# Eight memory query blocks moved from the stick-breaking stage's filler to the opening stage's quarter products

## The chip, the cores and the metric

The kernel runs on one core of a Trainium2 chip. TensorE (PE) multiplies matrices, VectorE (DVE), ScalarE (ACT) and GpSimd (POOL) do the elementwise work, and SyncE (SP) issues the DMAs. Each engine works through its own list of instructions in order and waits for the others at semaphores. The metric is the time of one execution in microseconds (us), lower is better.

## What is computed

One decoder layer on 1024 tokens of width 1024, in float32. The input is normed (RMSNorm gives `u`) and multiplied by one combined matrix `w_in`; the columns of the product feed three branches:

```python
u = rms_norm(h, norm_mix_pre)
proj = u @ w_in
sb_qkv, z, xbc_raw, dt_raw, mem_q, gate_logits = jnp.split(proj, SPLIT_POINTS, axis=-1)
...  # stick-breaking attention on sb_qkv; SSD on z, xbc, dt
kv = rms_norm(mem, norm_mem) @ w_mem_kv          # cross-attention into 256 memory tokens
y_mem = softmax(mem_q @ k.T / 16) @ v
...  # three projections, merged by sigmoid gates, w_o, norm, residual, squared-ReLU MLP
# ssd_branch:
xbc = silu(causal_depthwise_conv(xbc_raw, conv_w, conv_b))      # 4 taps
y = ssd_chunked(...) * silu(z)
```

`w_in` is held as 96 blocks of 128 columns. Blocks 0 to 23 are q, k, v of the stick-breaking attention, 24 to 39 are `z`, 40 to 63 are `xbc`, 64 to 71 are `mem_q`, 72 to 95 are the gates.

## The kernel before

Every float32 product is made of three passes over rounded halves (`split3`: high times high, high times low, low times high), so that a full product of one block of `w_in` with all 1024 tokens is 8 x 3 x 2 = 48 matmuls of 128x512.

**The opening stage** (`front`). DVE norms ten tiles of 128 tokens (eight of `x`, two of the memory). For tile i these are `invert(i)` (L854 and L858: the reciprocal and the scaled tile), then PE's `turn(i)` (L553, eight transposes), `scale_turned(i)` (L870), ACT's `round_u(i)` (L716), and `rest_of_u(i)` (L876). PE multiplies blocks 0 and 1 while the tiles come (`piece`, L562, two tiles at a time) and the dt columns (`decays`, L650), then sixteen memory items (`product_of_memory`, L576, 24 matmuls each). The weight of such an item is rounded by ACT (`round_kv`, L737) and its rest made by DVE (`rest_of_kv`, L894). Beside these items stand the four sums of `u` quarters that the next part multiplies (`round_t` L758 on ACT and `rest_of_t` L901 on DVE, in items 1 to 4), and after item 15 the first weights' halves (`round_front`, `round_back` L781, `rest_of_front` L905, `rest_of_back` L913).

Then come blocks 2 to 23 in eleven pairs. A pair is a 2 x 2 grid of quarters and is multiplied by seven quarter products in place of eight (`PRODUCTS`, L583): 7 x 4 x 3 = 84 matmuls of 128x512 a pair instead of 96. POOL makes four weight sums a pair, ACT rounds, DVE makes the rests and adds up the results.

**The stick-breaking stage** has 8 pairs of heads with 16 steps each, 128 steps in all. In step i, with t = i mod 8, PE multiplies scores on (t+1) x 128 columns (L1301); ACT takes two sigmoids (L1395 and L1399), DVE scans one of them (L1509), POOL multiplies (L1451), and in step i+2 PE transposes the result in one or two units (L1260), each of which ACT rounds (L1362) and DVE subtracts (L1459, `lo`). Every fourth step the values are weighed (L1317). PE transposes unit u only when DVE has finished unit u-2 (`pe.wait_ge(lo_done, u - 1)`).

Between these PE is filled with blocks of `w_in`: 48 blocks in the pattern `kinds = "xzxzxq"`, six to a pair of heads (L1279). The number of filler matmuls in a step is read from `AT_STEP`, by t. An x block goes through the convolution on DVE (`convolve`, four taps, L1469 and three times L1473, in the first and second step after the block's end), a sigmoid on ACT three steps after, a multiplication on DVE four steps after (`silu`, L1479), and a store by SP five steps after. A z block's two halves get a sigmoid from ACT (L1380) and a multiplication from DVE (`silu_of_gate`, L1484) in the step in which they end. A q block (`mem_q`) is copied by ACT (L1378) and stored. POOL splits the weights of each block (L1429, L1437). Results go through the two slots of `out_tile`, slot m mod 2 for filler block m: before, x blocks always have slot 0 and z and q blocks slot 1. A block may write its slot only when the block two before it has been stored.

After this stage come the SSD, the merge and the MLP, which the change doesn't touch.

## Time and profile before

| | |
|---|---|
| time, median of 3 runs | 2694.46 us (2691.84 to 2698.86) |
| the profiled execution | 2688.13 us, its span 2686.4 us |
| PE / DVE / ACT / POOL busy, of the span | 97% / 69% / 44% / 49% |
| granted clock of PE, mean | 0.99 |

In the profile a line such as L1279 is a line of the kernel before; "busy" of matmuls counts each until its modelled end, so a group's mean of 0.40 us is not the distance between two matmuls in a row. The chain that ended last is given by the page as PE for most of its length.

### The profile page before, as it was taken

The numbers are of one execution on the slowest core, as the hardware profiler recorded it, in microseconds if no ns is written. First come the engines' busy times: TensorE is split into PE (matmuls) and PEld (weight loads), VectorE is DVE, ScalarE is ACT, GpSimd is POOL, SyncE is SP. The second block draws the span as 40 slices with busy tenths as digits, with TensorE's granted clock in tenths as the row PEclk, the third lists the DMA queues.
The fourth block names the chain that finished last, engine by engine and source line by source line (L and its number), as shares of the span: only waits on it lengthen the run. The fifth ranks groups of instructions, "written<-read, shape, count | busy, mean of one in ns | idle before, by whom it ended". The sixth has DMA issues, their size and how long they took to land. (4 is left out here: it accounts for less than half of the span.)

```text
span 2686.4 us, 35512 instructions
## 1 busy us (share of the span) xinstructions
PE 2597.0 (97%) x12752; PEld 2175.4 (81%) x12752; DVE 1850.0 (69%) x2063; ACT 1191.2 (44%) x2098; POOL 1313.1 (49%) x809
## 2 busy tenths in 40 slices
PE   7999999999999999799999899999998999999998
PEld 6888888888888888688888777878887788888886
DVE  5666476777677677498888656653258887768567
ACT  5533144444444444467666544443144222244443
POOL 3233255454554554288888743545600676535224
PEclk9999999999999999899999999999999999999999
DMA  4634443433324341467666653434331444376574
GB/s 160 204 151 160 153 149 105 126 102 109 112 94 134 110 119 62 137 175 210 196 207 202 226 189 133 152 134 149 126 126 55 150 160 166 129 245 211 203 253 146
DMA packets 208108, 411.53 MB, mean 153 GB/s; under 512 B 19648, under 2 KB 100160, under 8 KB 207936
## 3 DMA queue, kind: packets, MB, share of 16 engines
q1 hardware_dynamic: 207936, 409.27, 46.0%
q8 instruction: 104, 1.70, 0.3%
q14 instruction: 68, 0.56, 0.1%
HBM read 289.01 MB, written 120.19 MB: 152 GB/s over the span
## 5 line engine op out<-in xcount | busy, mean ns | idle before, releaser
L1451 POOL TENSOR_TENSOR sb_beta<-sb_beta,sb_rest 128x128 f32<-128x128 f32 (+7 forms) x128 | 164.1, 1282 | 371.4 <-DVE sb_rest L1509 371.4
L1279 PE MATMUL sb_psg<-uh,sb_wl 128*128 128x512 f32 x768 | 309.7, 403 | 0.0
L1279 PE MATMUL sb_psg<-ul,sb_wh 128*128 128x512 f32 x768 | 304.3, 396 | 0.0
L1279 PE MATMUL sb_psg<-uh,sb_wh 128*128 128x512 f32 x768 | 302.8, 394 | 0.0
L3169 PE MATMUL ff_ps<-ff_mh,ff_total 128*128 128x512 f32 x896 | 278.6, 391 | 4.6 <-DVE ff_total L3672 4.6
L1509 DVE TENSOR_TENSOR_SCAN sb_rest<-sb_rest 128x128 f32<-128x128 f32 (+7 forms) x128 | 187.3, 1463 | 115.1 <-ACT sb_rest L1395 114.8
L3169 PEld LDWEIGHTS ff_ps<-ff_mh,ff_total 128*128 128x128 f32 x896 | 169.4, 189 | 41.0 <-issue 5.7
L2314 PE MATMUL first_ps<-uh,mg_wh 128*128 128x512 f32 x480 | 193.3, 403 | 6.2 <-DVE ul L2519 4.9
L2314 PE MATMUL first_ps<-ul,mg_wh 128*128 128x512 f32 x480 | 188.5, 393 | 0.0
L2314 PE MATMUL first_ps<-uh,mg_wl 128*128 128x512 f32 x480 | 188.3, 392 | 0.0
L3169 PE MATMUL ff_ps<-ff_ml,ff_total 128*128 128x512 f32 x448 | 175.2, 391 | 0.0
L1362 ACT ACTIVATE sb_wth<-sb_pst 128x512 fp32r<-128x512 f32 (+1 forms) x192 | 87.3, 490 | 189.9 <-PE sb_pst L1260 186.6
L1279 PEld LDWEIGHTS sb_psg<-ul,sb_wh 128*128 128x128 f32 x768 | 144.4, 188 | 29.9
L1279 PEld LDWEIGHTS sb_psg<-uh,sb_wl 128*128 128x128 f32 x768 | 144.6, 188 | 25.4
L1279 PEld LDWEIGHTS sb_psg<-uh,sb_wh 128*128 128x128 f32 x768 | 144.9, 189 | 24.0
L1801 PE MATMUL first_ps<-uh,ssd_gwh 128*128 128x512 f32 x384 | 155.0, 404 | 5.9 <-ACT ssd_out L1866 5.0
L1801 PE MATMUL first_ps<-ul,ssd_gwh 128*128 128x512 f32 x384 | 151.5, 395 | 0.0
L1801 PE MATMUL first_ps<-uh,ssd_gwl 128*128 128x512 f32 x384 | 151.2, 394 | 0.0
L1459 DVE TENSOR_TENSOR sb_wtl<-sb_pst,sb_wth 128x512 fp32r<-128x512 f32 (+1 forms) x192 | 99.6, 546 | 74.3 <-ACT sb_wth L1362 74.3
L2292 POOL TENSOR_TENSOR merged<-merged,mg_gate 128x1024 f32<-128x1024 f32 x24 | 61.3, 2553 | 159.6 <-DVE mg_gate L2526 159.6
L1473 DVE SCALAR_TENSOR_TENSOR sb_out<-sb_padded,sb_cw,sb_out 128x1024 f32<-128x1024 f32 x72 | 131.7, 1829 | 1.7
L1395 ACT ACTIVATE sb_rest<-sb_psz 128x128 f32<-128x128 f32 (+7 forms) x128 | 83.6, 653 | 108.6 <-PE sb_psz L1301 107.7
(422 smaller groups left out, 7259.6 us busy)
## 6 DMA issues: line engine op xcount, KB each, us to landing
sb_w<-in_w_in SPq DMA_DIRECT2D x48, 512.0 KB, 4.4
scratch_proj<-sb_out SPq DMA_DIRECT2D x48, 512.0 KB, 2.9
ff_w<-in_w_down SPq DMA_DIRECT2D x96, 256.0 KB, 3.4
sb_k<-scratch_qk SPq DMA_DIRECT2D x64, 256.0 KB, 6.1
ssd_arow<-scratch_decay SPq DMA_DIRECT2D x32, 512.0 KB, 5.6
mg_gate<-scratch_proj SPq DMA_DIRECT2D x32, 512.0 KB, 3.6
ff_w<-in_w_up SPq DMA_DIRECT2D x32, 512.0 KB, 3.7
mg_w<-in_w_branch SPq DMA_DIRECT2D x30, 512.0 KB, 4.5
```

The costliest lines, as they stand in the source:

```text
L1279: last = nc.tensor.matmul(ps_g[:, h], l[:, s, k], r[:, k, h * HALF:(h + 1) * HALF], start=(k == 0 and j == 0), stop=(k == KB - 1 and j == 2))
L1362: nc.scalar.activation(out, src, ACT.Copy).then_inc(hi_done, 1)
L1395: nc.scalar.activation(rest[:, i % 3, 1:cols + 1], ps_z[:, 0:cols], ACT.Sigmoid, scale=-0.125).then_inc(keep_done, 1)
L1451: nc.gpsimd.tensor_tensor(beta[:, i % 3, 0:cols], beta[:, i % 3, 0:cols], rest[:, i % 3, 0:cols], ALU.mult).then_inc(weighted, 1)
L1459: nc.vector.tensor_tensor(out, src, hi, ALU.subtract).then_inc(lo_done, 1)
L1473: nc.vector.scalar_tensor_tensor(out_tile[:, 0], padded[:, tap:tap + S], cw[:, n, tap:tap + 1], out_tile[:, 0], ALU.mult, ALU.add).then_in ...
L1509: nc.vector.tensor_tensor_scan(kept, kept, kept, 1.0, ALU.mult, ALU.bypass).then_inc(scanned, 1)
L1801: last = nc.tensor.matmul(ps_g[:, h], l[:, s, k], r[:, k, h * HALF:(h + 1) * HALF], start=(k == 0 and j == 0), stop=(k == KB - 1 and j == 2))
L2292: nc.gpsimd.tensor_tensor(merged[:, n % KB], merged[:, n % KB], gate[:, n % 2], ALU.add).then_inc(summed, 1)
L2314: last = nc.tensor.matmul(ps[:, s, cols], l[:, k], r[:, k, cols], start=(k == 0 and j == 0), stop=(k == KB - 1 and j == 2))
L3169: done = nc.tensor.matmul(down_bank(p, local), l[:, columns(local)], r, start=(begins and c == 0 and j == 0), stop=(c == PAIRS - 1 and j = ...
```

## The change

Three things are changed.

1. The eight `mem_q` blocks leave the filler and become four more pairs of the opening stage, after the eleven of before. The filler has 40 blocks in the pattern `"xzxxz"`, five to a pair of heads, with 8 to 22 matmuls a step in place of 11 to 25. `padded` gets a second buffer, and x and z blocks now use both slots of `out_tile`.
2. DVE norms tiles in another order: `scale_turned(i)`, `invert(i+1)`, `rest_of_u(i)`, and the third tile's `invert` stands behind the first two `rest_of_u`.
3. Memory items: the rest of weight 2 is made before the results of blocks 0 and 1 are rounded off; the four sums of `u` are rounded in items 2, 5, 8 and 11, behind the item's weight; the first pair's front factor is rounded in item 13 in place of 15, and its S1, S2 and S3 in item 14 in place of after 15.

```diff
-    BLOCK_PAIRS = [(b, b + 1) for b in range(2, Z0, 2)]
+    BLOCK_PAIRS = [(b, b + 1) for b in (*range(2, Z0 + Z_EARLY, 2), *range(MQ0, G0, 2))]
+    T_ITEMS = (2, 5, 8, 11)
...
+        round_kv(2)
         hi_of_first(0)
-        round_kv(2)
...
-            if m == 15:
+            if m == 13:
                 round_front(0)
+            if m == 14:
+                for which in (S1, S2, S3):
+                    round_back(which, 0)
...
-    kinds = "xzxzxq"
+    kinds = "xzxxz"
-    AT_STEP = (11, 13, 15, 17, 19, 21, 23, 25)
+    AT_STEP = (8, 10, 12, 14, 16, 18, 20, 22)
...
-                if kind != "x" and m >= 2:
+                if kind == "z" and m >= 2:
                     act.wait_ge(g_stored[s], (m // 2) * 16)
...
-                    if n:
-                        dve.wait_ge(g_stored[0], n * 16)
-                    nc.vector.tensor_scalar(out_tile[:, 0], padded[:, 0:S], cw[:, n, 0:1], cb[:, n:n + 1],
+                    if m >= 2:
+                        dve.wait_ge(g_stored[s], (m // 2) * 16)
+                    nc.vector.tensor_scalar(out_tile[:, s], padded[:, n % 2, 0:S], cw[:, n, 0:1], cb[:, n:n + 1],
```

(`Z_EARLY` is 0.) How this stands in the engines' lists is shown at three places.

DVE, steps 14, 15 and 16 of the second pair of heads (L1509 in before and L1522 after are the scans, of 896, 1024, 128 and then 256 columns; L1459 and L1472 are `lo`; L1469, L1473 and L1482, L1486 the taps). Before:

```order
L1509 SCALAR_TENSOR_TENSOR sb_rest<-sb_rest 128x896 [waits sb_keep]
L1459 TENSOR_TENSOR sb_wtl<-sb_pst,sb_wth 128x4x128 [waits sb_hi]
L1459 TENSOR_TENSOR sb_wtl<-sb_pst,sb_wth 128x128 [waits sb_hi]
L1469 TENSOR_SCALAR sb_out<-sb_padded,sb_cw,sb_cb 128x1024 [waits sb_gstored0,sb_drained1,sb_drained0]
L1473 SCALAR_TENSOR_TENSOR sb_out<-sb_padded,sb_cw,sb_out 128x1024 [waits sb_convstep]
L1493 TENSOR_TENSOR sb_y<-sb_psy,sb_y 64x512 [waits sb_yupper,sb_ydone]
L1509 SCALAR_TENSOR_TENSOR sb_rest<-sb_rest 128x1024 [waits sb_keep]
...
L1473 SCALAR_TENSOR_TENSOR sb_out<-sb_padded,sb_cw,sb_out 128x1024 [waits sb_convstep] x2
L1509 SCALAR_TENSOR_TENSOR sb_rest<-sb_rest 128x128 [waits sb_keep]
L1459 TENSOR_TENSOR sb_wtl<-sb_pst,sb_wth 128x4x128 [waits sb_hi]
```

After:

```order
L1522 SCALAR_TENSOR_TENSOR sb_rest<-sb_rest 128x896 [waits sb_keep]
...
L1492 TENSOR_TENSOR sb_out<-sb_out,sb_sigm 128x1024 [waits sb_sigm]
L1482 TENSOR_SCALAR sb_out<-sb_padded,sb_cw,sb_cb 128x1024 [waits sb_gstored0,sb_drained1,sb_drained0]
L1486 SCALAR_TENSOR_TENSOR sb_out<-sb_padded,sb_cw,sb_out 128x1024 [waits sb_convstep]
L1497 TENSOR_TENSOR sb_out<-sb_psg,sb_out 128x512 [waits sb_zsigm0]
L1506 TENSOR_TENSOR sb_y<-sb_psy,sb_y 64x512 [waits sb_yupper,sb_ydone]
L1522 SCALAR_TENSOR_TENSOR sb_rest<-sb_rest 128x1024 [waits sb_keep]
...
L1486 SCALAR_TENSOR_TENSOR sb_out<-sb_padded,sb_cw,sb_out 128x1024 [waits sb_convstep] x2
L1497 TENSOR_TENSOR sb_out<-sb_psg,sb_out 128x512 [waits sb_zsigm1]
L1522 SCALAR_TENSOR_TENSOR sb_rest<-sb_rest 128x128 [waits sb_keep]
L1472 TENSOR_TENSOR sb_wtl<-sb_pst,sb_wth 128x4x128 [waits sb_hi]
```

A silu (L1492) and the two gate multiplications of a z block (L1497) now stand in these steps; before they held the same four taps, but neither of those.

ACT, steps 14 and 15 of the second pair of heads. L1395, L1399 and L1408, L1412 are the two sigmoids, L1362 and L1376 the rounding of the transposed units. Before:

```order
L1395 ACTIVATE sb_rest<-sb_psz 128x896 [waits sb_weighted,sb_scores]
L1399 ACTIVATE sb_beta<-sb_psz 128x896 [waits sb_turned]
L1362 ACTIVATE sb_wth<-sb_pst 128x4x128 [waits sb_ydone,sb_turned]
L1362 ACTIVATE sb_wth<-sb_pst 128x128 [waits sb_turned]
L1417 ACTIVATE sb_y<-sb_psy 64x512 [waits sb_ydone]
L1395 ACTIVATE sb_rest<-sb_psz 128x1024 [waits sb_weighted,sb_scores]
```

After:

```order
L1408 ACTIVATE sb_rest<-sb_psz 128x896 [waits sb_weighted,sb_scores]
L1412 ACTIVATE sb_beta<-sb_psz 128x896 [waits sb_turned]
L1376 ACTIVATE sb_wth<-sb_pst 128x4x128 [waits sb_ydone,sb_turned]
L1376 ACTIVATE sb_wth<-sb_pst 128x128 [waits sb_turned]
L1392 ACTIVATE sb_out<-sb_psg 128x512 [waits sb_gstored1,sb_halfdone]
L1430 ACTIVATE sb_y<-sb_psy 64x512 [waits sb_ydone]
L1408 ACTIVATE sb_rest<-sb_psz 128x1024 [waits sb_weighted,sb_scores]
```

The sigmoid of the z block's first half (L1392) now stands in step 14 and waits for the store (`gstored1`) of the x block whose silu DVE does in the same step 14.

DVE, the norm of the third and fourth tile. Before:

```order
L876 TENSOR_TENSOR ul<-fr_f_hi,uh 128x8x128 [waits fr_uhi] x2
L854 RECIPROCAL fr_stats<-fr_stats 128x1 [waits fr_rooted]
L858 TENSOR_SCALAR fr_f_sums<-fr_f_back,fr_stats 128x1024 [waits fr_turned,fr_inverted]
L870 TENSOR_TENSOR fr_f_hi<-fr_ps,fr_gains 128x1024 [waits fr_uhi,fr_rawkept,fr_usplit,fr_turned]
L876 TENSOR_TENSOR ul<-fr_f_hi,uh 128x8x128 [waits fr_uhi]
```

After:

```order
L881 TENSOR_TENSOR ul<-fr_f_hi,uh 128x8x128 [waits fr_uhi]
L859 RECIPROCAL fr_stats<-fr_stats 128x1 [waits fr_rooted]
L863 TENSOR_SCALAR fr_f_sums<-fr_f_back,fr_stats 128x1024 [waits fr_turned,fr_inverted]
L875 TENSOR_TENSOR fr_f_hi<-fr_ps,fr_gains 128x1024 [waits fr_uhi,fr_rawkept,fr_usplit,fr_turned]
L859 RECIPROCAL fr_stats<-fr_stats 128x1 [waits fr_rooted]
L863 TENSOR_SCALAR fr_f_sums<-fr_f_back,fr_stats 128x1024 [waits fr_turned,fr_inverted]
L881 TENSOR_TENSOR ul<-fr_f_hi,uh 128x8x128 [waits fr_uhi]
```

The next tile's reciprocal and scaling now stand between a tile's `scale_turned` (L875) and its `rest_of_u` (L881).

## Rows read from the trace of the kernel before

**Rows 1.** Windows: stretch, length, busy (count) of PE, PEld, DVE, ACT, POOL; clock, DMA:
```profile
126.24:336.50 210.26, 209.89 (x924) 173.47 (x925) 128.35 (x156) 63.70 (x91) 62.80 (x42) 1.00 0.43 153
338.99:1097.14 758.15, 752.81 (x3830) 633.31 (x3828) 541.82 (x519) 341.17 (x616) 377.87 (x222) 1.00 0.35 108
```

**Rows 2.** Waits of PE in the opening stage: sum of us, times, longest:
```profile
PE fr_ps L562 <- DVE ul L876: 6.8, 3, 4.4
PE fr_ps L583 <- DVE fr_fl L905: 2.8, 1, 2.8
PE fr_ps L576 <- DVE fr_fl L894: 2.6, 2, 2.4
...
PE fr_ps L583 <- DVE fr_back L913: 0.4, 1, 0.4
```

**Rows 3.** Waits of PE from 345 to 1088 us, all there are:
```profile
PE sb_psy L1317 <- DVE sb_wtl L1459: 0.4, 1, 0.4
```

**Rows 4.** The chain that ended last, a stretch of 128x512 matmuls only:
```profile
2366.69 259.09 PE ff_ps L3169 x1143
```

**Rows 5.** Timeline of PE in the opening stage: start, duration, instruction, idle before it:
```profile
46.59 0.48 PE L562 MATMUL fr_ps<-uh,fr_fh 128*128 128x256 f32 x1 [1.90 <-DVE ul L876]
...
51.07 1.03 PE L553 MATMUL fr_ps<-ident,fr_f_sums 128*128 128x128 f32 x8
51.86 0.36 PE L562 MATMUL fr_ps<-uh,fr_fh 128*128 128x256 f32 x1
...
54.82 1.04 PE L553 MATMUL fr_ps<-ident,fr_f_sums 128*128 128x128 f32 x8
```

**Rows 6.** Timeline of DVE in the opening stage:
```profile
24.83 1.23 DVE L876 TENSOR_TENSOR ul<-fr_f_hi,uh 128x1024 fp32r<-128x1024 f32 x1 [1.12 <-ACT uh L716]
...
64.84 1.22 DVE L894 TENSOR_TENSOR fr_back<-fr_w,fr_back 128x1024 fp32r<-128x1024 f32 x1
...
72.69 4.48 DVE L894 TENSOR_TENSOR fr_fl<-fr_w,fr_fh 128x1024 fp32r<-128x1024 f32 x1
```

**Rows 7.** Timeline of DVE, steps 14 to 16 of the second pair of heads:
```profile
512.94 0.89 DVE L1459 TENSOR_TENSOR sb_wtl<-sb_pst,sb_wth 128x512 fp32r<-128x512 f32 x2 [1.91 <-ACT sb_wth L1362]
513.75 2.39 DVE L1469 TENSOR_SCALAR sb_out<-sb_padded,sb_cw,sb_cb 128x1024 f32<-128x1024 f32 x1
516.17 1.28 DVE L1473 SCALAR_TENSOR_TENSOR sb_out<-sb_padded,sb_cw,sb_out 128x1024 f32<-128x1024 f32 x1
...
521.33 3.65 DVE L1473 SCALAR_TENSOR_TENSOR sb_out<-sb_padded,sb_cw,sb_out 128x1024 f32<-128x1024 f32 x2
...
525.23 1.13 DVE L1459 TENSOR_TENSOR sb_wtl<-sb_pst,sb_wth 128x512 fp32r<-128x512 f32 x2
```

**Rows 8.** Timeline of PE: the score of step 14, the transposes in step 17:
```profile
506.93 0.39 PE L1301 MATMUL sb_psz<-sb_k,sb_q 128*128 128x512 f32 x1
...
527.77 1.04 PE L1260 MATMUL sb_pst<-ident,sb_beta 128*128 128x128 f32 x8
```

**Rows 9.** DVE lines from 350 to 1088 us: duration ns min/median/max:
```profile
L1479 DVE TENSOR_TENSOR sb_out<-sb_out,sb_sigm x23: 1298/2183/2729, 380.2 to 1060.6; 128x1024 f32<-128x1024 f32 x23
```
```profile
L1484 DVE TENSOR_TENSOR sb_out<-sb_psg,sb_out x32: 676/680/685, 362.2 to 1062.0; 128x512 f32<-128x512 f32 x32
```

**Rows 10.** Timeline of DVE: a silu, and a tap that waits for its store:
```profile
380.17 2.33 DVE L1479 TENSOR_TENSOR sb_out<-sb_out,sb_sigm 128x1024 f32<-128x1024 f32 x1
...
385.61 0.81 DVE L1469 TENSOR_SCALAR sb_out<-sb_padded,sb_cw,sb_cb 128x1024 f32<-128x1024 f32 x1 [0.36 <-DMA scratch_proj<-sb_out]
```

**Rows 11.** Groups from 350 to 1088 us: ACT's sigmoid of half a z block:
```profile
L1380 ACT ACTIVATE sb_out<-sb_psg 128x512 f32<-128x512 f32 x32 | 19.1, 598 | 30.0 <-PE sb_psg L1279 30.0
```

**Rows 12.** Timeline of POOL in steps 14 and 15 of the second pair of heads:
```profile
513.19 2.39 POOL L1437 TENSOR_TENSOR sb_wl<-sb_w,sb_wh 128x1024 fp32r<-128x1024 f32 x1
```

**Rows 13.** Timeline of PE: after idling, at the first quarter product:
```profile
126.24 0.47 PE L583 MATMUL fr_ps<-uh,fr_fh 128*128 128x512 f32 x1 [2.77 <-DVE fr_fl L905]
126.54 0.40 PE L583 MATMUL fr_ps<-ul,fr_fh 128*128 128x512 f32 x1
```

99 lines of the change are left out of this document (53 added, 46 removed).

## Prediction, made before the changed kernel ran

> **What bounds the kernel now.** I read first the windows of the two stages that the change touches. In the quarter products PE is busy for 209.89 of 210.26 us, and in the stick-breaking stage for 752.81 of 758.15 us [rows 1]. Then the waits of PE: within the 128 steps, from 345 to 1088 us, it waited once, for 0.4 us [rows 3]. So PE sets the length of both stages, and a matmul taken out is worth its distance to the next one. That distance is best read from a long stretch without a wait: 1143 matmuls in 259.09 us [rows 4], 0.2267 us each. In the opening stage PE does wait: 6.8 us for the rests of `u`, 2.6 us for the rest of a memory weight, 2.8 and 0.4 us for the first factors [rows 2]. DVE is the second engine: 541.82 us of work in the 758.15 us of the stick-breaking stage [rows 1], so 71%. An average says little about it, since its work comes in lumps, and I look at one lump below.
>
> **Matmuls.** The eight blocks take 8 x 48 = 384 matmuls out of the filler, and four pairs add 4 x 84 = 336 to the opening. The difference is 48 x 0.2267 = 10.9 us less. By stages: 384 x 0.2267 = 87.1 us leave the stick-breaking stage and 76.2 us enter the opening. The four new pairs need no more of DVE, ACT and POOL than the eleven before did, which kept DVE busy for 128 and POOL for 63 of 210 us [rows 1], and they aren't split for the attention; their cover is ample, and I put the rest of them at nothing. ACT loses sixteen copies and POOL sixteen weight splits in the later stage; neither engine was waited for, so this is nothing on the path.
>
> **Norms.** Each `rest_of_u` waited about 1.12 us for ACT ([rows 6] show one of nine alike); the next tile's `invert` now stands in that gap. PE gains only where it waited for DVE. Against it: PE's list has `turn(2)` before the first piece, and `turn(2)` needs the third `invert`, which now stands behind the second `rest_of_u`. The first piece waited 4.4 us for that rest [rows 2] and now waits also for the `invert` and the transposes, some 2.6 us more. Then the wait of 1.90 us at 46.59 should go, and with it the slow piece behind it: that one took 51.07 - 46.59 = 4.48 us, the next one like it 54.82 - 51.86 = 2.96 [rows 5], because after idling PE ran at the lower clock. Together +2.6 - 1.9 - 1.5 and -0.4 for the third wait: about -1.2 us.
>
> **Memory items.** The rest of weight 2 took from 72.69 to 77.17 [rows 6], though the same line takes 1.22 us at 64.84; POOL's two long sums of `u` ran beside it. It now stands one place earlier, so of the 2.4 us that PE waited I take 1 us off, with some 0.8 of slow clock. The 2.8 and 0.4 us before the quarter products [rows 2] go, since the factors are ready in items 13 and 14; no slow matmuls followed them (0.30 us from one to the next) [rows 13], so it is 3.2 us. What is late next is the product itself, that is nothing. The opening without the matmuls gains 1.2 + 1.8 + 3.2 = 6 us. Bounds: 3 us, if DVE gives back the norm's part at the start, and 9 us, if both the late rests and the slow clock behind them vanish.
>
> **The filler's pattern, in step 14 of every pair of heads.** Here I expect the cost. With five blocks to 16 steps, the silu of the third block (x) falls into step 14, beside the first two taps of the fourth block, and the fifth block (z) has its two gate multiplications in steps 14 and 15. Before, these steps held the taps alone. The waiting instruction is PE's transpose in step 17: it needs DVE's `lo` of a unit of step 16, and that `lo` is queued behind all the lumps. From the score of step 14 to those transposes PE takes 527.77 - 506.93 = 20.84 us [rows 8]. DVE has the first `lo` of step 16 done at about 525.23 + 0.68 = 525.91 [rows 7], where 0.68 is the duration of 128x512 from PSUM [rows 9], 18.98 us after the same score. The margin is 1.9 us.
>
> After the change PE comes earlier: three filler matmuls less in each of the steps 14, 15 and 16 and one less in the first half of 17, 10 x 0.2267 = 2.3 us. DVE is busy without a gap over 0.1 us from 512.94 to this `lo`, thirteen instructions, of which [rows 7] show the first and the last units and three of the taps, but starts that run 0.3 us earlier. To its queue come a silu and two gate multiplications, 2 x 0.68 = 1.36 us. The silu takes 1.30 us at the least and 2.18 in the median [rows 9]. So the wait is at least 1.36 + 1.30 + 2.3 - 1.9 - 0.3 = 2.8 us, and with a silu of 2.7 us, the slowest, 4.2.
>
> On top comes the store. ACT's sigmoid of the z block's first half writes the slot of the x block whose silu has just been done. From the end of a silu to the start of a tap that waits for its store, the trace has 385.61 - 382.50 = 3.1 us [rows 10]; the sigmoid adds 0.6 [rows 11], 3.7 in all. Meanwhile DVE does two taps, between 2.1 and 3.7 us (tap 0 took 2.39 and 0.81, tap 1 took 1.28) [rows 7, 10]. So 0 to 1.6 us more, during which both engines stand still; behind ACT's waiting instruction are the copy of y and the sigmoids of step 15, behind DVE's the scan of step 15. The whole is 2.8 to 5.8 us, and I take 4.0, near the median silu and the middle of the store's share. It comes once per pair of heads, eight times: 32 us, from 22 to 46. In step 10 the values are weighed right behind a step of 1024 columns; my margin there comes out within half a us of nothing, and I add 0.4 us each, 3 us (0 to 12). Nothing is made up later, since PE has no idle time to give back.
>
> A rule bears on the silu. In the trace, the tap at 513.75 took 2.39 us against 0.81 at its quickest, and POOL's rest of a weight ran from 513.19 to 515.58 [rows 7, 10, 12]. The Trainium skill (SBUF — State Buffer, section "SBUF: two separate sides") says why: one port pair shared by GpSimd and VectorE is an exclusive lock, and whichever starts first holds it for the whole instruction. The trace agrees with it. If the silu starts ahead of POOL's rest, it costs 1.3 us and the stage pays 8 x 2.8 = 22 us; if it starts behind, 8 x 4.2 = 34.
>
> **The sum** against the profiled execution: 2688.1 - 10.9 - 6 + 35 = 2706 us. PE now idles for 2 us at a time in the stage. After 1.90 us it came back slow [rows 5], after 2.77 it didn't [rows 13]; a slow stretch costs 1.5 us, so 0 to 12 us for eight, and I take 3: 2709. The profiled execution lies 6.3 us under the median of the runs, and this is carried over: **2715 us**.
>
> **Rivals.** First: DVE keeps up. It has 216 us of idle time in the stage [rows 1], of which 87 go, and POOL holds the shared ports for sixteen long instructions less. If the taps and the silu run at their quickest (a tap 0.8 to 1.3 in place of 1.8 on average), the critical queue is 3 us shorter and the wait falls below 0.5 us. It decides at a margin of nothing in step 17. Then 2694.5 - 10.9 - 6 = 2678 us, 2671 to 2686, faster. Against it: POOL's splits in steps 14 and 15 remain where they were. Second: the queue shrinks by half of this, with 1 to 2 us a pair of heads, and the two effects cancel: 2678 + 8 to 2678 + 20, say 2692. Third: the store's wait comes in full, the clock drops at each of the waits, and step 10 pays too: 2678 + 46 + 12 + 8 = 2744 us.
>
> **How the numbers follow.** Forecast, 2700 to 2730: 0.48. DVE keeps up: 0.20. Cancelling, 2686 to 2700: 0.19. Everything in full, above 2730: 0.13. A measurement of this kernel tells about 0.3%, 8 us, from no change. Below 2686.4 lies the first rival, 0.20; between 2686.4 and 2702.5 the second and the lower edge of the forecast, 0.23; above it 0.57. A range for 8 in 10 leaves out most of the first rival and the top of the third: 2682 to 2745.
>
> **What would show it.** The changed profile should have the quarter products at 15 pairs x 84 matmuls with PE busy throughout (about 286 us) and no wait for the first factors. In the stick-breaking stage the steps without waits would take 671 us; I expect about 706, and waits of L1260's line (the transposes) for DVE's `lo` eight times at 2 us or more, with a second, shorter kind: scores waiting for ACT's sigmoid, behind a wait of ACT for the store. The forecast is wrong if PE's waits there sum to under 10 us, or if they stand elsewhere than in steps 16 and 17 of a pair of heads.

## The result, and the profile after

The changed kernel takes 2752.61 us in the median (2748.23 to 2763.69), the kernel before 2693.77 us in the same comparison: a ratio of 1.0222, 95% interval 1.0188 to 1.0255. It is 59 us slower; the forecast was 21 us slower, and the range ended at 2745. The profiled execution took 2753.5 us with a span of 2751.8 us; the mean granted clock fell from 0.990 to 0.981.

Windows of the kernel after, in the columns of [rows 1]: the quarter products, then the stick-breaking stage.

```profile
128.40:415.66 287.26, 287.26 (x1269) 237.93 (x1268) 165.29 (x211) 81.11 (x117) 81.93 (x58) 1.00 0.40 144
415.70:1157.10 741.40, 691.62 (x3449) 572.27 (x3447) 550.20 (x519) 331.84 (x600) 357.54 (x206) 0.97 0.33 100
```

The quarter products are what the forecast said: from the first of them at 128.26 to the first filler matmul at 413.89 it is 285.6 us, with PE busy throughout (the first window also holds eight filler matmuls that stand ahead of the first score). The first score comes at 415.70 in place of 338.99: 76.7 us later. The added matmuls are 76.2 of it, and three filler matmuls fewer stand ahead of it (8 in place of 11), 0.7 us. So the opening itself is 1.2 us slower, and its -6 us isn't there. Behind the first score 381 matmuls are gone, 86.4 us; from the first score to the start of the last weighing matmul the stick-breaking stage fell from 757.9 to 741.2 us only. It lost 69.7 us on its bare sum, where 38 had been forecast. The waits of PE in it, from 420 to 1150 us (sum, times, longest), stand where [rows 3] had one of 0.4 us:

```profile
PE sb_pst L1274 <- DVE sb_wtl L1472: 23.7, 16, 3.5
PE sb_psy L1331 <- DVE sb_wtl L1472: 14.0, 8, 1.9
PE sb_psz L1315 <- ACT sb_beta L1412: 8.4, 7, 2.6
```

L1274 are the transposes, L1331 the weighing of the values, L1315 the scores; L1472 is the remainder (`lo`) on DVE, L1412 the second sigmoid on ACT. The first and the third line are the forecast's two kinds of wait. The second, 14.0 us, was put at 3. The first line holds two waits of 1.9 and 3.5 us that stand behind the last score, at the stage's end; the 128 steps themselves have 18.3 us in 14 waits of the transposes, and 40.7 us of waits in all.

**A table by step.** For all later readings I took PE's start of each score (step i), the distance to the next score, and its difference to the same distance in the trace before, with 0.2267 us added for each filler matmul that the step no longer has. What is left is what a step costs beyond its work: waits, and matmuls at the lower clock. Sums over all pairs of heads, in us, by the step's number in a pair of heads (16 steps); "ends" is what the stage lost between its first score and step 2, and after the last score. Steps 16 and 17 of a pair of heads are steps 0 and 1 of the next. A small negative number stands where the kernel before lost a little itself. e1 has the stage of before and e2 the stage of after, so they show how far two profiled executions of the same stage differ: 0.1 us in the steps and 3.2 at the ends for e1, 1.8 and 1.0 for e2.

```
                    step 0     1     2     6     9    10    13    14    15  rest   sum  ends  median us
after                  7.3  18.3   3.3   0.0   0.0  19.9   0.2   1.9   9.6   0.1  60.6   9.1     2752.6
e1  new orders         0.0   0.0   0.0   0.0   0.0   0.1   0.0   0.0   0.0   0.0   0.1   3.2     2695.2
e2  move only          7.1  20.3   2.8   0.0   0.0  19.9   0.2   1.7   9.8   0.5  62.4   8.1     2752.9
e3  third slot        11.5  23.9   2.9   0.0   0.0  18.3   0.2   1.8   0.1   1.0  59.7   6.5     2749.9
e4  two taps          13.3   0.7   1.6   0.0   0.0   7.9   0.3  -0.3  13.7   3.6  40.8   5.3     2726.9
e5  silu later         2.0  36.6   3.2   0.0   0.0   6.3   0.2   1.8   0.1   1.7  51.9   6.0     2745.3
e6  spread             3.8   7.6  17.7   0.0   0.0  15.7   0.2  -0.3   0.1   0.1  44.9   4.5     2736.0
e7  flat              40.8   0.2   0.0  11.3   2.9  -1.1   0.0  -0.2   0.0  -0.4  53.5   7.6     2745.9
e8  flat, spread       5.7   6.5  10.2   1.0   0.4  -1.1   0.0  -0.2   0.0  -0.3  22.2   6.0     2715.4
e9  zxxzx              1.7   0.1   0.8  -0.1   0.1  -1.1   0.0  -0.2   0.0  -0.4   0.9   6.6     2691.5
e10 xzxzx, mild       -0.1   0.0   0.0   0.0   9.2  -1.1   0.0  -0.1   0.1  -0.1   7.9   6.9     2700.6
e11 the two tables    -0.1   0.0   3.3   7.2   5.9  -1.0   0.1  -0.1   0.1  -0.4  15.0   5.1     2702.5
e12 e8, two taps      -0.1   0.1   0.0   1.4   0.1  -1.1   0.0  -0.2   0.0  -0.4  -0.2   4.1     2688.4
e13 e9, old norms      1.7   0.1   0.7  -0.1   0.1  -1.1   0.0  -0.2   0.0  -0.4   0.8   6.5     2687.0
e14 e13, end           1.7   0.2   0.7  -0.1   1.0  -0.9   0.0   0.6   0.0   0.3   3.5   3.8     2688.0
e15 kinds alone       -0.2   0.0   5.2   0.0   0.0  16.0   7.2   0.0   0.1   4.1  32.4   8.1     2722.1
e16 filler alone      12.2  12.1   3.9   5.5   5.9  -1.0   0.0  -0.1   0.2  -0.4  38.3   6.0     2732.8
```

**Steps 14 to 17.** The timelines of the second pair of heads (start, duration, instruction, idle before it). The score of step 15 started at 584.98, that of step 16 at 594.46 and that of step 17 at 598.17. DVE and POOL first:

```profile
584.23 2.24 DVE L1492 TENSOR_TENSOR sb_out<-sb_out,sb_sigm 128x1024 f32<-128x1024 f32 x1
586.39 2.89 DVE L1482 TENSOR_SCALAR sb_out<-sb_padded,sb_cw,sb_cb 128x1024 f32<-128x1024 f32 x1
589.31 1.28 DVE L1486 SCALAR_TENSOR_TENSOR sb_out<-sb_padded,sb_cw,sb_out 128x1024 f32<-128x1024 f32 x1
591.77 0.69 DVE L1497 TENSOR_TENSOR sb_out<-sb_psg,sb_out 128x512 f32<-128x512 f32 x1 [1.17 <-ACT sb_out L1392]
...
583.26 2.12 POOL L1464 TENSOR_TENSOR sb_beta<-sb_beta,sb_rest 128x896 f32<-128x896 f32 x1 [1.96 <-DVE sb_rest L1522]
585.34 3.38 POOL L1450 TENSOR_TENSOR sb_wl<-sb_w,sb_wh 128x1024 fp32r<-128x1024 f32 x1
```

Then ACT and PE:

```profile
591.13 0.60 ACT L1392 ACTIVATE sb_out<-sb_psg 128x512 f32<-128x512 f32 x1 [7.58 <-DMA scratch_proj<-sb_out]
...
593.30 1.02 ACT L1412 ACTIVATE sb_beta<-sb_psz 128x1024 f32<-128x1024 f32 x1
...
594.46 0.30 PE L1315 MATMUL sb_psz<-sb_k,sb_q 128*128 128x128 f32 x1 [2.58 <-ACT sb_beta L1412]
...
596.45 0.95 PE L1274 MATMUL sb_pst<-ident,sb_beta 128*128 128x128 f32 x7 [0.50 <-DVE sb_wtl L1472]
...
601.86 1.06 PE L1274 MATMUL sb_pst<-ident,sb_beta 128*128 128x128 f32 x8 [2.02 <-DVE sb_wtl L1472]
```

Silu, tap and tap fill DVE from 584.23 to 590.59. The sigmoid of the z block stands on ACT for 7.58 us, to the end, until the store of the silu's block has landed; the two sigmoids of step 15 are queued behind it, and the scores of step 16 wait 2.58 us for them. Then DVE is late with its remainders, and the transposes of steps 16 and 17 wait. That is the forecast's chain, link by link. The silu began 1.1 us ahead of POOL's rest of a weight, and was slow (2.24 us) all the same, since POOL's product of 583.26 ran until 585.38; the tap behind it then met the rest (2.89 us).

The pair of heads shown is one of three in eight in which the store was late: 4.1 to 4.7 us from the silu's end to the start of the sigmoid, where the other five have 2.9 to 3.0, near the 3.1 of the forecast. Where it was late the scores waited 1.7 to 2.6 us, in the other pairs of heads 0.3 to 0.9. What makes these stores late isn't shown.

**Step 10.** DVE and POOL, then PE:

```profile
550.54 3.00 DVE L1492 TENSOR_TENSOR sb_out<-sb_out,sb_sigm 128x1024 f32<-128x1024 f32 x1
553.46 0.68 DVE L1522 TENSOR_TENSOR_SCAN sb_rest<-sb_rest 128x256 f32<-128x256 f32 x1
554.07 1.25 DVE L1472 TENSOR_TENSOR sb_wtl<-sb_pst,sb_wth 128x512 fp32r<-128x512 f32 x2
...
550.06 2.40 POOL L1450 TENSOR_TENSOR sb_wl<-sb_w,sb_wh 128x1024 fp32r<-128x1024 f32 x1
```
```profile
555.38 0.50 PE L1331 MATMUL sb_psy<-sb_wth,sb_v 128*128 128x512 f32 x1 [1.88 <-DVE sb_wtl L1472]
...
556.77 0.63 PE L1331 MATMUL sb_psy<-sb_wth,sb_v 128*128 128x512 f32 x1
557.20 0.63 PE L1331 MATMUL sb_psy<-sb_wtl,sb_v 128*128 128x512 f32 x1
```

The silu of the first block (8 + 10 + 12 + 14 filler matmuls fall short of its 48, so it ends in step 4, and its silu is in step 8) began 0.48 us after POOL's rest of a weight and took 3.00 us; the same line takes 1.2 at its quickest. The scan and the remainders of step 9 are queued behind it, and the weighing of step 10 needs those remainders. The Trainium skill (SBUF — State Buffer, section "SBUF: two separate sides") says that the shared port pair is held for a whole instruction; the trace agrees, the silu's end at 553.54 being 1.1 us past the end of POOL's instruction. Eight weighings wait 1.65 to 1.88 us. Three of the eight then run at half rate (0.43 us from one matmul to the next, the 1.2 GHz level), and take 4.7 us in place of 3.2.

**The opening.** Its waits of PE, against [rows 2] and 11.5 us in 3 waits of the transposes L553 before:

```profile
PE fr_ps L555 <- DVE fr_f_sums L863: 22.6, 7, 9.4
PE fr_ps L578 <- ACT fr_kvout L745: 2.2, 1, 2.2
PE fr_ps L578 <- DVE fr_fl L899: 1.8, 1, 1.8
PE fr_ps L564 <- DVE ul L881: 1.1, 1, 1.1
```

Timelines of DVE and POOL in it:

```profile
34.62 1.82 DVE L863 TENSOR_SCALAR fr_f_sums<-fr_f_back,fr_stats 128x1024 f32<-128x1024 f32 x1
36.36 2.29 DVE L881 TENSOR_TENSOR ul<-fr_f_hi,uh 128x1024 fp32r<-128x1024 f32 x1
...
34.59 1.30 POOL L498 TENSOR_TENSOR fr_f_t<-fr_f_hi,fr_f_t 128x512 f32<-128x512 f32 x1 [11.24 <-DVE fr_f_hi L875]
35.84 1.73 POOL L498 TENSOR_TENSOR fr_f_t<-fr_f_hi 128x512 f32<-128x512 f32 x1
```

The waits for the rests of `u` fell from 6.8 to 1.1 us, as intended, and those of the transposes doubled. Of their 22.6 us, 8.2 are one wait at the third tile, which the forecast had foreseen: the first piece starts 2.6 us later (24.44 against 21.86). New besides it are four waits of 0.2, 1.3, 0.9 and 1.3 us. `invert` (L863) and `rest_of_u` (L881), which take 0.75 and 1.22 us alone, now start together with POOL's sums and take 1.82 and 2.29 for four tiles; in the kernel before they took at most 1.59 and 1.33 for these. The first memory matmul is 3.35 us late (71.88 against 68.53); the quarter products then start without a wait, as forecast, and are 2.0 us late (128.26 against 126.24).

### The profile page after: what moved, and what is told of

It reads as the page before. It is cut to its first block and busy times, and to the rows that moved or that the text cites. A ratio compares the mean times of both kernels' runs of the same rounds, so it can differ in the third digit from the quotient of the medians.

```text
span 2751.8 us, 35549 instructions
## 1 busy us (share of the span) xinstructions
PE 2612.1 (95%) x12704; PEld 2179.0 (79%) x12704; DVE 1903.0 (69%) x2115; ACT 1200.9 (44%) x2110; POOL 1312.0 (48%) x809
## 5 line engine op out<-in xcount | busy, mean ns | idle before, releaser
L1293 PE MATMUL sb_psg<-ul,sb_wh 128*128 128x512 f32 x640 | 261.2, 408 | 0.0
L1293 PE MATMUL sb_psg<-uh,sb_wh 128*128 128x512 f32 x640 | 257.5, 402 | 0.0
L1293 PE MATMUL sb_psg<-uh,sb_wl 128*128 128x512 f32 x640 | 254.0, 397 | 0.0
L1522 DVE TENSOR_TENSOR_SCAN sb_rest<-sb_rest 128x128 f32<-128x128 f32 (+7 forms) x128 | 196.1, 1532 | 65.4 <-ACT sb_rest L1408 65.1
L1376 ACT ACTIVATE sb_wth<-sb_pst 128x512 fp32r<-128x512 f32 (+1 forms) x192 | 87.8, 491 | 187.6 <-PE sb_pst L1274 183.4
L1472 DVE TENSOR_TENSOR sb_wtl<-sb_pst,sb_wth 128x512 fp32r<-128x512 f32 (+1 forms) x192 | 99.5, 545 | 96.1 <-ACT sb_wth L1376 96.1
L1293 PEld LDWEIGHTS sb_psg<-uh,sb_wh 128*128 128x128 f32 x640 | 121.6, 190 | 23.1
L1293 PEld LDWEIGHTS sb_psg<-uh,sb_wl 128*128 128x128 f32 x640 | 121.7, 190 | 22.0
L1293 PEld LDWEIGHTS sb_psg<-ul,sb_wh 128*128 128x128 f32 x640 | 121.8, 190 | 19.6
L1408 ACT ACTIVATE sb_rest<-sb_psz 128x128 f32<-128x128 f32 (+7 forms) x128 | 83.9, 655 | 114.2 <-PE sb_psz L1315 114.0
L1486 DVE SCALAR_TENSOR_TENSOR sb_out<-sb_padded,sb_cw,sb_out 128x1024 f32<-128x1024 f32 x72 | 129.6, 1799 | 1.7
```

The source lines that it names most:

```text
L1293: last = nc.tensor.matmul(ps_g[:, h], l[:, s, k], r[:, k, h * HALF:(h + 1) * HALF], start=(k == 0 and j == 0), stop=(k == KB - 1 and j == 2))
L1376: nc.scalar.activation(out, src, ACT.Copy).then_inc(hi_done, 1)
L1408: nc.scalar.activation(rest[:, i % 3, 1:cols + 1], ps_z[:, 0:cols], ACT.Sigmoid, scale=-0.125).then_inc(keep_done, 1)
L1472: nc.vector.tensor_tensor(out, src, hi, ALU.subtract).then_inc(lo_done, 1)
L1486: nc.vector.scalar_tensor_tensor(out_tile[:, s], padded[:, n % 2, tap:tap + S], cw[:, n, tap:tap + 1], out_tile[:, s], ALU.mult, ALU.add). ...
L1522: nc.vector.tensor_tensor_scan(kept, kept, kept, 1.0, ALU.mult, ALU.bypass).then_inc(scanned, 1)
```

## The experiments

### The parts of the change (e1, e2)

**e1** is the kernel before with the new orders alone; **e2** is the kernel after with the old ones.

```diff
 e1, against after:
-    BLOCK_PAIRS = [(b, b + 1) for b in (*range(2, Z0 + Z_EARLY, 2), *range(MQ0, G0, 2))]
+    BLOCK_PAIRS = [(b, b + 1) for b in range(2, Z0, 2)]
 (and stick_breaking as in before)
```

> The kernel before with only the second and third part of the change: the norms of the opening and the sixteen memory items in their new order on the vector and scalar engine. The query blocks stay in the projection filler, so the stick-breaking stage is that of before. The prediction gave these two parts -6 us (-3 to -9), which would be a time of about 2688. In the trace after, the memory matmuls began 3.35 us later than before (71.88 against 68.53) and the waits within the items were 3.2 us fewer, so the theory now is that the two cancel: 2690 to 2697, no measurable change. Rival: the moves of the opening cost something that the trace after hides, and this kernel is slower than before by 5 us or more.

> The changed kernel with the norms and memory items in the order of the kernel before: only the query blocks move, and the filler of the stick-breaking stage is xzxxz. If the whole loss stands in the stick-breaking stage (742 us after, against a bare sum of about 671), this kernel is as slow as the changed one, 2748 to 2756. Rival: the opening and its order share in the loss (through what it leaves late for the stage behind it), and then this one is 5 us or more below the changed one.

Measured: e1 2695.21 against 2694.47 us, ratio 1.0003 (0.9993 to 1.0013); e2 2752.93 us, ratio 1.0214 (1.0199 to 1.0229). The new orders are worth nothing, in either surrounding, and the whole loss is in the move of the query blocks. e1 shows something else: from the first matmul behind the stick-breaking stage to the end it takes 1581.4 us and the kernel after 1581.0, where the profiled execution of before has 1575.5 with the same code. All the other profiled executions of this case have 1579.0 to 1587.5 there. So the 6.3 us by which that execution lay under its median were mostly there, and to carry them over was right.

### The store (e3)

```diff
-            sp.dma_start(proj[row_of(m)], out_tile[:, m % 2]).then_inc(g_stored[m % 2], 16)
+            sp.dma_start(proj[row_of(m)], out_tile[:, m % 3]).then_inc(g_stored[m % 3], 16)
...
-                    act.wait_ge(g_stored[s], (m // 2) * 16)
+                    act.wait_ge(g_stored[m % 3], (m // 3) * 16)
```

> The changed kernel, with three slots in place of two for the finished projection blocks (out_tile), so that no gate and no convolution waits for the store of the block two before. Theory: the store stands behind the silu of its block, and ScalarE's gate sigmoid of step 14 waits for it (7.58 us in the trace after), which delays the sigmoids of step 15 and the score matmuls of step 16 (10.2 us of TensorE waits in 8). With a third slot these waits go, those for the vector engine in steps 10, 16 and 17 stay: 8 to 12 us below the changed kernel, about 2742. Rival: the store is hidden, the vector engine alone sets the pace there, and the time stays within 3 us of the changed kernel.

Measured: 2749.88 us, 1.0192 (1.0172 to 1.0212). The waits of PE from 420 to 1150 us:

```profile
PE sb_pst L1275 <- DVE sb_wtl L1473: 29.7, 15, 4.1
PE sb_psy L1332 <- DVE sb_wtl L1473: 15.6, 9, 1.9
PE sb_psz L1316 <- ACT sb_beta L1413: 0.9, 1, 0.9
```

The wait did what I expected, and the time didn't. The scores no longer wait (step 15: 9.6 to 0.1), but steps 0 and 1 now cost 35.4 in place of 25.6: what PE had waited for ACT, it waits a step later for DVE, whose queue is as long as before. The rival holds: 3 us less, which isn't clear of the two intervals (1.0172 to 1.0212 against 1.0188 to 1.0255). The Trainium skill (Perfetto Trace Analysis, section "Optimization Strategy") says that the same gap repeating on the engine that should be saturated can mean too few buffers. Here a gap that came in every pair of heads and was released by a buffer's store went with a third buffer, and 7.3 of the 7.5 us that it took away within the steps came back as waits of the transposes for DVE.

### DVE's work, and where it stands (e4, e5, e6)

```diff
 e4 (the counts of conv_step to match):
                 if kind_of(m) == "x" and i == end + 2:
-                    convolve(m, range(2, CONV))
+                    pass
 e5, on e3 (its store one step later too):
-                if kind_of(m) == "x" and i == end + 4:
+                if kind_of(m) == "x" and i == min(end + 5, EVENTS - 1):
                     silu(m)
 e6, on e3 (sigmoid at +5, silu at +6, store at +7):
-                if kind_of(m) == "x" and i == end + 1:
-                    convolve(m, range(2))
-                if kind_of(m) == "x" and i == end + 2:
-                    convolve(m, range(2, CONV))
+                if kind_of(m) == "x" and 1 <= i - end <= CONV:
+                    convolve(m, range(i - end - 1, i - end))
```

> The changed kernel with the last two of the four taps of each convolution left out (48 operations of the vector engine fewer, part of what is computed is gone); the filler of TensorE, its order and all else stay. Theory: what costs the time is the vector engine's lumps (taps and silu packed before the remainders of steps 10, 16 and 17). With the taps of the second step gone the waits of transposes and weighing for the remainders (39 us in 25) shrink to those for the silu, the clock stays full, and the time falls by 25 to 45 us, to 2708 to 2728. Rival: eight filler matmuls at the first step are simply too few to cover the chain score, sigmoid, scan, product, transpose, whatever the vector engine does besides; then the time moves by less than 10 us.

Measured: 2726.91 us, 1.0112 (1.0088 to 1.0135), 26 us less, within what was expected. The waits from 420 to 1150 us:

```profile
PE sb_psz L1315 <- ACT sb_beta L1412: 14.4, 8, 2.2
...
PE sb_psy L1331 <- DVE sb_wtl L1472: 8.2, 9, 1.4
PE sb_pst L1274 <- DVE sb_wtl L1472: 5.8, 8, 1.7
```

The waits for remainders fell from 37.7 to 14.0 us. With DVE less late, the store's wait costs more than it did: 27.0 us in steps 15 and 0 against 16.9, of them 12.5 as waits for ACT, 3.0 as waits for DVE and most of the rest as slow matmuls behind these. (The eighth wait for ACT is in step 3 of the first pair of heads.) A window of the second pair of heads, right behind such a wait, shows the granted clock (the last but two) at 0.50:

```profile
592.50:594.60 2.10, 2.10 (x8) 1.71 (x7) 1.51 (x3) 1.76 (x3) 0.56 (x2) 0.50 0.99 349
```

> The changed kernel with three slots for finished blocks, and each convolution's closing product (silu) and its store one step later, so that in step 8 of each pair of heads the vector engine makes the remainder before the silu. Theory: the wait of the weighing in step 10 (step 10 costs 19.9 us over all pairs of heads in the changed kernel, 18.3 with the third slot) is the silu of step 8 alone; it falls to below 3 us, and the time by 12 to 18 us against the kernel with the third slot, to 2732 to 2738, with steps 1, 15 and 16 as they are there (35 us). Rival: the lump only moves, the next remainder is as late, and the gain is under 5 us.

Measured: 2745.33 us, 1.0186 (1.0158 to 1.0215), 4.6 us under e3, not clear of the intervals; the table has 7.8 less in the steps. The silu in step 8 was most of step 10's cause: it fell from 18.3 to 6.3. But the third block's silu now stands in step 15 and pushes the taps of the fourth:

```profile
589.22 2.33 DVE L1493 TENSOR_TENSOR sb_gap<-sb_gap,sb_sigm 128x1024 f32<-128x1024 f32 x1
591.47 2.60 DVE L1487 SCALAR_TENSOR_TENSOR sb_gap<-sb_padded,sb_cw,sb_gap 128x1024 f32<-128x1024 f32 x2
...
595.73 1.94 PE L1275 MATMUL sb_pst<-ident,sb_beta 128*128 128x128 f32 x8 [3.21 <-DVE sb_wtl L1473]
```

Step 1 rose from 23.9 to 36.6. The rival's words, "the lump only moves", describe the time, and the theory's the place.

> The changed kernel with three slots, and the vector engine's work on a block spread out: one tap in each of the four steps behind the block, the sigmoid in the fifth, the silu in the sixth, all of it computed, no operation fewer. Filler and order of TensorE stay. Theory (the lumps, not the work, cost the time): steps 0, 1 and 15 lose most of their 35 us, and 20 to 35 us are gained against the kernel with the third slot: 2715 to 2730. Rival (the vector engine has too much work there, however it is packed): under 8 us gained.

Measured: 2735.95 us, 1.0158 (1.0138 to 1.0179), 13.9 us under e3, between the two expectations. Steps 0 and 1 fell from 35.4 to 11.4, as they should; step 2 rose from 2.9 to 17.7. The two places that are left look alike. For step 10 of the second pair of heads it is a tap in step 8, where the silu has gone, and it took 3.00 us beside POOL's rest of a weight; for step 2 it is step 0, where a silu and a tap stand ahead of the remainders that its weighing needs.

```profile
547.69 3.00 DVE L1487 SCALAR_TENSOR_TENSOR sb_gap<-sb_padded,sb_cw,sb_gap 128x1024 f32<-128x1024 f32 x1
...
547.22 2.40 POOL L1451 TENSOR_TENSOR sb_wl<-sb_w,sb_wh 128x1024 fp32r<-128x1024 f32 x1
...
593.31 1.21 DVE L1493 TENSOR_TENSOR sb_gap<-sb_gap,sb_sigm 128x1024 f32<-128x1024 f32 x1
594.44 1.28 DVE L1487 SCALAR_TENSOR_TENSOR sb_gap<-sb_padded,sb_cw,sb_gap 128x1024 f32<-128x1024 f32 x1
```

### The cover (e7, e8)

```diff
-    AT_STEP = (8, 10, 12, 14, 16, 18, 20, 22)
+    AT_STEP = (15,) * TB
```

> The changed kernel with 15 filler matmuls in every step in place of 8 to 22; nothing else changes. The steps that wait (0, 1, 2) then have 7, 5 and 3 matmuls more beside the same chain, and the last steps of each head fewer. Theory (cover): 1.6 and 1.1 us more cover in steps 0 and 1 take away about 1 us in each of the 8 places where step 1 waits 2.3, the store is no longer late, and the silu falls in other steps: 10 to 25 us gained, 2727 to 2742. Rival: the pattern of blocks against steps makes the lumps, the waits move to other steps, and the time stays within 8 us of the changed kernel.

Measured: 2745.86 us, 1.0192 (1.0172 to 1.0213), 7 us less, not clear of the intervals: the rival. Steps 1, 10 and 15 lose nothing now, step 6 loses 11.3 and step 0 loses 40.8. A new wait stands in step 0 (DVE, then PE, behind the second pair of heads), 17.9 us in seven:

```profile
585.24 3.28 DVE L1486 SCALAR_TENSOR_TENSOR sb_out<-sb_padded,sb_cw,sb_out 128x1024 f32<-128x1024 f32 x1
588.44 0.68 DVE L1497 TENSOR_TENSOR sb_out<-sb_psg,sb_out 128x512 f32<-128x512 f32 x1
...
589.26 0.47 PE L1293 MATMUL sb_psg<-uh,sb_wh 128*128 128x512 f32 x1 [2.72 <-DVE sb_out L1497]
```

The filler itself waits for the gate product that frees its PSUM bank, and the gate is queued behind a tap that took 3.28 us.

> The one-tap-a-step order with three slots and 15 filler matmuls in every step together. Theory: both causes are then gone, cover and lumps, and what is left of the stage is its bare sum of about 671 us plus 5 to 12 us: 2690 to 2705. Rival: the waits only move (to the weighing, whose remainders share their steps with a tap), and it is no better than the better of the two alone.

Measured: 2715.36 us, 1.0081 (1.0056 to 1.0107). The expectation was missed by 10 us, but the two edits, 14 and 7 us apart, give 34.5 together (against 2749.88, with the third slot). 22.2 us are left, in steps 0, 1 and 2.

### How much of it is DVE (e12)

It is e8 without the last two taps of every convolution.

> The flat and spread kernel with xzxxz, and the last two of the four taps of every convolution left out (48 operations of the vector engine fewer, part of what is computed is gone). It asks how much of the 22 us that are left there is still the vector engine's. Theory: all but the gates and the silu of step 2: step 0 and 1 fall to under 2 us each, step 2 stays, and the time comes 8 to 12 us below the flat and spread kernel, 2703 to 2707. Rival: the waits left are those of the chain itself with too little filler beside it, and fewer taps gain under 4 us.

Measured: 2688.43 us, 0.9979 (0.9969 to 0.9988), 27 us less. The steps cost nothing any more (-0.2). With the same filler and the same chain of score, sigmoid, scan and product, all the 22 us of e8 went with half of the taps, so they were DVE's queue; 15 filler matmuls a step are cover enough for the chain alone. (e15 below shows the same for 8 and 10 matmuls: nothing is lost in steps 0 and 1.) The expectation had left step 2 its 10 us: wrong.

### The kinds against the steps (e9, e10)

```diff
-    kinds = "xzxxz"
-    PER = len(kinds)
+    PER = 5
+    kinds = "zxxzx" * (SB_PAIRS - 1) + "zxxxz"
```

> The flat and spread kernel (three slots, one tap a step, 15 filler matmuls in every step) with the kinds of blocks in the order zxxzx in place of xzxxz (the last pair of heads zxxxz). Blocks end in steps 3, 6, 9, 12 and 15 of a pair of heads, so the gates, which are two operations of VectorE in the steps where a block ends, leave step 15, and no silu falls in step 2, where the weighing waits 10.2 us over all pairs of heads in the kernel with xzxxz. Theory (which operations meet which step decides, to the single one): of the 22 us that the steps 0, 1 and 2 lose there, step 2 gives back most of its 10.2 and step 0 some of its 5.7; 8 to 15 us gained, 2700 to 2707. Rival (the steps 0 to 2 are short of cover whatever stands beside them): under 4 us gained.

> As the kernel with zxxzx, but with the kinds in the order xzxzx (the last pair of heads xzxxz) and 12, 13, 14, 15, 15, 16, 17 and 18 filler matmuls in the eight steps of a head in place of 15 in each. Theory: with the operations kept out of the steps 15 to 2, the cover of the first steps matters less, and this is as good as zxxzx within 5 us: 2697 to 2707. Rival (cover of the first steps): steps 0 and 1, with 3 and 2 matmuls fewer, lose 5 to 10 us more than with the flat filler.

Measured: e9 2691.50 us, 0.9995 (0.9985 to 1.0004); e10 2700.56 us, 1.0026 (1.0016 to 1.0036). One string moved 24 us between e8 and e9, more than expected; nothing is computed less. From 420 to 1080 us e9 has no wait of PE at all. Its window of the stage:

```profile
417.20:1094.80 677.60, 669.08 (x3442) 562.10 (x3440) 567.77 (x519) 331.10 (x600) 345.57 (x206) 0.99 0.36 108
```

DVE is busy for 84% of the stage and PE doesn't wait for it in these steps; in the changed kernel it is busy for 74%, and PE waits 40.7 us in them. e10 came as expected in time. Its loss is in step 9 (9.2 us), not in steps 0 and 1, where it has less cover than e9: again no sign of the rival.

### The two tables apart and together (e11, e15, e16)

```diff
 e11 (e15: the kinds alone, e16: AT_STEP alone)
-    kinds = "xzxxz"
-    PER = len(kinds)
+    PER = 5
+    kinds = "xzxzx" * (SB_PAIRS - 1) + "xzxxz"
-    AT_STEP = (8, 10, 12, 14, 16, 18, 20, 22)
+    AT_STEP = (12, 13, 14, 15, 15, 16, 17, 18)
```

> The changed kernel with two slots and its taps two a step as they are, and only two tables of numbers other: the kinds xzxzx (the last pair of heads xzxxz) and 12, 13, 14, 15, 15, 16, 17, 18 filler matmuls. Theory: the meeting of lumps and steps explains about half of the 61 us that the steps lose in the changed kernel; this one keeps the lumps and moves them, and comes to 2710 to 2725. Rival: lumps cost the same wherever they fall, and it stays above 2738.

> The changed kernel with one thing other: the kinds of a pair of heads in the order xzxzx (the last xzxxz) in place of xzxxz. The filler stays at 8 to 22 matmuls, the taps two a step, the slots two. It and the kernel with the milder filler alone split the 50 us that both together gave. Theory: the order gives the larger part, 20 to 35 us, 2718 to 2733. Rival: without cover in steps 0 and 1 the order gives under 15 us.

> The changed kernel with one thing other: 12, 13, 14, 15, 15, 16, 17 and 18 filler matmuls in the steps of a head in place of 8 to 22; the kinds stay xzxxz. Theory: 4 and 3 matmuls more in steps 0 and 1 are 0.9 and 0.7 us of cover, in 8 pairs of heads 10 to 20 us off what they lose, 2733 to 2743; the lumps behind blocks stay, and step 10 with them. Rival: as with 15 in every step (7 us gained there), the lumps come to lie elsewhere and it gains under 8 us.

Measured: e11 2702.46 us, 1.0039 (1.0024 to 1.0055); e15 2722.12 us, 1.0113 (1.0098 to 1.0128); e16 2732.82 us, 1.0146 (1.0133 to 1.0159). e11 came 8 us below what was expected of it, e15 as expected, and e16 at the edge. The kinds alone give back 30.5 us, the filler alone 19.8, both 50.1. No operation is other, no slot added; with two tables of numbers, 50 of the 59 us are gone. Each leaves what the other takes: e15 has no loss in steps 0, 1 and 15 but keeps 16.0 in step 10, e16 has none in step 10 (its expectation had kept it) but keeps 24.3 in steps 0 and 1.

### Can the move be made to pay (e13, e14)

e13 is e9 with the norms in the order of before and the memory items in the new one; e14 is e13 with `xxxzz` as the last five kinds.

```diff
 e13, against e9:
+        for i in range(TILES + 2):
+            if i >= 3:
+                rest_of_u(i - 2)
+            if i < TILES:
+                invert(i)
+            if 0 < i <= TILES:
+                scale_turned(i - 1)
...
 e14, against e13:
-    kinds = "zxxzx" * (SB_PAIRS - 1) + "zxxxz"
+    kinds = "zxxzx" * (SB_PAIRS - 1) + "xxxzz"
```

> The kernel with zxxzx, flat filler, three slots and one tap a step, with the norms of the opening in the order of the kernel before and only the memory items in their new order. Theory: the two halves of the opening's reorder cancel (the norms cost 3.35 us up to the first memory matmul, the items save 3.2 us of waits behind it), so the old norms with the new items give 2 to 4 us against the kernel with both new: 2687 to 2690, which is faster than the kernel before by 3 to 6 us. Rival: what the norms lose, the loads and the items behind them wait out anyway, and the difference is under 1 us.

> The kernel of e13 with the kinds of the last pair of heads xxxzz in place of zxxxz, so that the last silu is over before the last remainders, where TensorE's transposes wait 4.0 us. Theory: 2 to 4 us less than e13, 2684 to 2688. Rival: the stage's end is set by the store of y and the loads behind it, or the remainders are late by the two gates instead, and the difference is under 1 us.

Measured: e13 2686.99 us against 2693.76, ratio 0.9980 (0.9971 to 0.9989); e14 2687.99 us, 0.9984 (0.9975 to 0.9992). By the medians e13 is 6.8 us faster than the kernel before (2.4 to 7.8 by the interval of the ratio), 66 us faster than the changed one, and does the whole computation. Its first quarter product starts at 125.05, its first score at 414.08, 3.1 us before that of e9; but e14, which has the same opening, has its own at 127.60 and 416.62, so one profiled execution of each doesn't tell what the old norms give. Its window of the stage:

```profile
414.08:1091.50 677.42, 668.89 (x3442) 561.94 (x3440) 567.69 (x519) 330.94 (x600) 345.56 (x206) 0.99 0.36 108
```

In e14 the stage's ends fell from 6.5 to 3.8 us, and its steps rose from 0.8 to 3.5, all of it in the steps 8, 9, 10 and 14 of the last pair of heads. The two cancel: a lump was moved once more.

## Why the prediction was wrong

The direction and the forecast's one place were right, the size wasn't, and the time lies above the range. By the traces, the change costs 76.7 - 16.7 = 60 us up to the end of the stick-breaking stage. The forecast's sum for the same was -10.9 - 6 + 35 + 3 = 21 us. Four steps of it failed: step 10, the slow clock, the stage's end, which had no term, and the opening's gain. Term by term:

- **Matmuls, -10.9 us.** Right. The quarter products took 285.6 us against 286 forecast, and in e9 the steps cost 0.9 us beyond the bare sum.
- **Norms, -1.2 us.** Wrong in sign: the first memory matmul came 3.35 us later. The +2.6 us at the first piece came as forecast, and so did the -1.9 and -1.5 for the wait at 46.59 and the slow piece behind it. The step that failed is "the next tile's `invert` now stands in that gap". POOL's sums run in the gap too; `invert` and `rest_of_u` get slower beside them, and the transposes have the four new waits, 3.7 us. I had counted DVE's idle time and not POOL's instructions in it. ("One of nine alike" was misread too: in the trace before, seven of the ten rests waited 1.12 or 1.13 us, one 1.53 and two not at all.) Over all profiled executions the first memory matmul comes at 70.4 to 72.7 in the fourteen with the new norms and at 67.6 to 69.9 in the four with the old ones.
- **Memory items, -5.0 us** (1.8 for the third rest, 3.2 for the first factors). Right in kind, too large: the wait before the quarter products went, but new waits of 1.8 and 2.2 us stand among the items. From the first memory matmul to the first quarter product it is 57.7 us before and in e2, and 54.9 to 57.8 in the sixteen executions with the new items, so 0 to 2.8 us less. Both orders together gave +1.2 us and not -6.
- **Steps 14 to 17, 32 us.** Mechanism and size were right: the waits for ACT and those of the transposes are 26.6 us in seven places, 3.8 us in each where 4.0 had been forecast. The eighth place is the stage's end, below. Only the store's share was wrong as a price. The forecast added it to DVE's lateness; e3 shows that they overlap, since without the store the steps gain 0.9 us. That the price still comes out is partly luck.
- **Step 10, 3 us (0 to 12).** The waits alone are 14.0 us. I had put the margin "within half a us of nothing" by the width of the step, and had looked for a silu only in step 14. The first block's silu falls into step 8, beside POOL's rest of a weight, ahead of just the remainders that step 10 needs. e5, which moves that silu, takes 12 us off the step; with a tap in its place (e6) the step is back at 15.7.
- **Slow clock, 3 us (0 to 12).** Too small. The steps lose 60.6 us and the waits in them sum to 40.7. Of the 19.9 us between, 11.6 are 61 matmuls of 128x512 that stand 0.36 us or more apart, at or near the lower level, behind waits; the rest isn't divided further (the first matmuls behind a wait, other shapes, pauses too short for the views). The forecast counted one slow stretch in each of eight waits at a chance; there are 29 waits in the steps. Step 10 has 5.9 us of it, where three weighings of eight lose 1.6 us each.
- **The stage's end, not costed.** 9.1 us with the stage's first steps (1.1 there, 7.9 at the end); e1, with the stage of before, has 1.6 and 1.6, so not all of it is the change's. After the last score nothing but filler and then nothing at all covers the last x block's taps and silu, which stand ahead of the last remainders:

```profile
1142.88 1.57 PE L1274 MATMUL sb_pst<-ident,sb_beta 128*128 128x128 f32 x7 [1.90 <-DVE sb_wtl L1472]
1147.97 1.94 PE L1274 MATMUL sb_pst<-ident,sb_beta 128*128 128x128 f32 x8 [3.52 <-DVE sb_wtl L1472]
1151.32 0.79 PE L1331 MATMUL sb_psy<-sb_wth,sb_v 128*128 128x512 f32 x1 [1.41 <-DVE sb_wtl L1472]
...
1153.20 0.63 PE L1331 MATMUL sb_psy<-sb_wth,sb_v 128*128 128x512 f32 x1
1153.62 0.63 PE L1331 MATMUL sb_psy<-sb_wtl,sb_v 128*128 128x512 f32 x1
```

The last weighing came back at half rate and took 5.5 us in place of 3.1. Before, the two waits there were 1.5 and 1.6 us; the last block was a plain copy (q), with neither taps nor gates.

The misses are 7.2 (orders), -5.4 (steps 14 to 17), 11.0 (step 10), 16.9 (clock) and 9.1 (ends), together the 39 us. Of the rivals, "everything in full" (2744) had the right parts, but that it comes near is partly luck: its 46 us for steps 14 to 17 are more than the 26.6 found, and its opening gains 6 us. "DVE keeps up" (2678) isn't far from what the same move reaches with other tables (e9, e13), but it is DVE's order that decides, not the speed of its taps. The forecast's own test, waits elsewhere than in steps 16 and 17, struck in part: of the 46.1 us from 420 to 1150, 14.0 stand in step 10 and 5.4 behind the last score.

**What stays open.** No run takes POOL's instructions away from DVE's, so how much of the lumps is the shared port and how much their own length isn't divided; the slow taps and silus (silu: 1.2 to 3.4 us, 2.1 in the median in the changed kernel) only show that it is much. It isn't shown either why three of the eight stores came late. Nor is it shown why `zxxzx` fits best; e9 and e10 show that which operation meets which step decides, not a rule by which to choose.

## What to carry to other kernels

When a filler is cut or its blocks get another period, lay out every operation that hangs on a block's end (taps, silu, gates, store) against the steps, one full period of both, and look at the queue ahead of each thing that PE waits for, and at the end of the stage too; the step where a lump doubles is only one of them. Change the table that sets the pattern before buffers are added or work is taken away: here two tables gave 50 us, half the taps 26, and a third buffer 3, which isn't clear of the noise. A wait is worth only what isn't late behind it anyway, and an order that fills an engine's gap should be held against the other engine that shares its ports.
